# Another order for the first tiles of a hybrid encoder layer, and identity transposes on TensorE at the start

## The reference, cut to what matters

```python
h = rmsnorm(x, norm1_g)
proj = h @ w_in                          # 512 q, 128 k, 128 v, 512 u columns
q = axial_rope(rmsnorm(q, q_norm_g)); k = axial_rope(rmsnorm(k, k_norm_g))
a = attention(q, k, v)                   # 8 query heads, 2 key/value heads of 64, bidirectional
p = multiscale_pool(u, w_pool, pool_scale)      # 4 groups, windows 2, 4, 8, 16
x = x + concat(a, p) @ w_out
x = x + square(relu(rmsnorm(x, norm2_g) @ w_up)) @ w_down
```

## Time and profile before

| | us |
|---|---|
| median of 3 runs | 1545.71 (1545.16 to 1547.87) |
| profiled execution | 1550.65 |
| its span, first to last instruction | 1548.9 |
| PE busy | 1501.4 (97%) |
| DVE, ACT, POOL busy | 1033.5, 730.0, 391.6 |
| mean granted TensorE clock | 0.993 of 2.4 GHz |

### The profile page before, as it was taken

The page is one execution under the profiler, slowest core; times in us unless marked ns, Lnnn a source line. Parts: engine busy times, 40 slices in busy tenths (PEclk is TensorE's granted clock), DMA queues, the critical chain, the costliest instruction groups (busy, mean ns, idle before and its releaser), DMA issues.

```text
span 1548.9 us, 23445 instructions
## 1 busy us (share of the span) xinstructions
PE 1501.4 (97%) x8000; PEld 1333.6 (86%) x8000; DVE 1033.5 (67%) x1290; ACT 730.0 (47%) x1231; POOL 391.6 (25%) x337
## 2 busy tenths in 40 slices
PE   6999989999989998999999999999899999999998
PEld 5999877888868887999999999999688888888887
DVE  6533479999976567544544544447688878888875
ACT  5222269999882344545545545546233223223220
POOL 3432577888870001000000000000222311311300
PEclk9999999999999999999999999999999999999999
DMA  6110011000023745643243243247743443443434
GB/s 232 47 46 17 18 69 45 15 10 14 11 79 123 257 181 214 285 151 134 108 151 134 106 153 134 103 156 268 266 150 95 150 150 102 146 153 105 149 97 175
DMA packets 68789, 193.55 MB, mean 125 GB/s; under 512 B 5504, under 2 KB 7680, under 8 KB 68736
## 3 DMA queue, kind: packets, MB, share of 16 engines
q1 hardware_dynamic: 66832, 181.85, 33.4%
q10 hardware_dynamic: 1904, 11.01, 1.7%
HBM read 120.49 MB, written 67.63 MB: 121 GB/s over the span
## 4 chain that ended last, share of the span: by engine, by line
PE 82%; POOL 5%; DVE 4%; issue 3%; ACT 3%; DMA 2%; SPq 0%; ACTq 0%; POOLq 0%; DVEq 0%
PE ps L736 22%; PE ps L738 21%; PE ps L737 21%; PE ps L933 5%; PE ps L834 3%; PE ps L941 3%; POOL prob L2014 2%; DMA hin<-hd 2%; PE ps L849 1%; PE ps L850 1%; PE ps L816 1%; PE ps L818 1%; PE ps L951 1%; POOL sw_prompt L1957 1%; PE ps L745 1%
## 5 line engine op out<-in xcount | busy, mean ns | idle before, releaser
L736 PE MATMUL ps<-h,wuhi 128*128 128x384 f32 x896 | 300.2, 335 | 5.0 <-issue 3.8
L738 PE MATMUL ps<-h,wulo 128*128 128x384 f32 x896 | 299.9, 335 | 0.0
L737 PE MATMUL ps<-h,wuhi 128*128 128x384 f32 x896 | 299.9, 335 | 0.0
L736 PE MATMUL ps<-wdhi,hidhi 128*128 128x512 f32 x672 | 262.6, 391 | 5.9 <-DVE yacc L1854 5.9
L737 PE MATMUL ps<-wdlo,hidhi 128*128 128x512 f32 x672 | 262.2, 390 | 0.0
L738 PE MATMUL ps<-wdhi,hidlo 128*128 128x512 f32 x672 | 262.1, 390 | 0.0
L1854 DVE TENSOR_TENSOR yacc<-yacc,ps 128x1024 f32<-128x1024 f32 x168 | 204.2, 1217 | 82.5 <-PE ps L738 82.4
L1036 ACT ACTIVATE hidhi<-hin 128x1024 fp32r<-128x1024 f32 (+1 forms) x72 | 86.9, 1207 | 312.0 <-PE ps L738 299.1
L1769 DVE TENSOR_TENSOR u<-u,ps 128x384 f32<-128x384 f32 x96 | 53.1, 553 | 186.3 <-PE ps L738 186.2
L736 PEld LDWEIGHTS ps<-h,wuhi 128*128 128x128 f32 x896 | 168.7, 188 | 5.8 <-issue 5.8
L737 PEld LDWEIGHTS ps<-h,wuhi 128*128 128x128 f32 x896 | 168.7, 188 | 0.0
(11 more groups left out here) (171 smaller groups left out, 2892.7 us busy)
## 6 DMA issues: line engine op xcount, KB each, us to landing
hd<-hout SPq DMA_DIRECT2D x64, 384.0 KB, 3.3
hin<-hd SPq DMA_DIRECT2D x48, 512.0 KB, 3.7
hd<-hout SPq DMA_DIRECT2D x32, 576.0 KB, 2.8
hin<-hd SPq DMA_DIRECT2D x24, 768.0 KB, 4.4
wuraw<-in_w_up SPq DMA_DIRECT2D x17, 1024.0 KB, 6.0
wdraw<-in_w_down SPq DMA_DIRECT2D x8, 2048.0 KB, 9.4
h<-h2d ACTq DMA_DIRECT2D x7, 1536.0 KB, 12.5
xin<-in_x SPq DMA_DIRECT2D x12, 512.0 KB, 3.4
```

Of the source, the lines that this page charges most:

```text
L736: pe.matmul(out, w_hi, m_hi, start=start, stop=False, skip_group_check=resumed)
L737: pe.matmul(out, w_hi, m_lo, start=False, stop=False, skip_group_check=resumed)
L738: return pe.matmul(out, w_lo, m_hi, start=False, stop=stop, skip_group_check=resumed)
```

## The change

- SP: the order becomes x0, ident, w0, g1, w1, w2, w3, x1, w4 to w7, x2, the u columns, gqk, rope, x3, edge, pscale.
- PE: 14 transposes of the identity into an unused part of PSUM before `transpose_x(0)` and 6 behind it. Tile 0's projection (`first_qkv`) goes row by row through q, k and v together, rows 0 to 2 first without the low part of the tile; `transpose_x(1)` moves into it, behind row 4. Tile 1's projection (`second_qkv`) goes into banks 4 and 5, which are those of `project_u`, so it needs not wait for tile 0 to be copied out. `transpose_x(3)` moves from before `project_u(0)` to between its second and third group, `transpose_qk(0)` from there to before the fourth.
- ACT and DVE: rows 0 to 2 of the weights are split before tile 0, rows 4 to 7 before tile 1; the u columns are split in two halves, between the steps of tile 0. The order of the first pair is written out (`first_pair`).
- POOL: the memset of `up` goes between `norm_x(0)` and `norm_x(1)`; for tile 0 the norm of q and k goes before `norm_x(3)`. For tile 1 the order stays.
- The loops over blocks 0 and 1 are written out (Python's `for` instead of `Fori`) on PE, ACT, DVE and POOL.

```diff
+    def load_wi(k):
+        sp.dma_start(wraw[:, k, 0:QKVW], w_in[k * P:(k + 1) * P, 0:QKVW]).then_inc(w_in_in[k], 16)
     sp.dma_start(xin[:, 0], x[0:P]).then_inc(x_in[0], 16)
+    sp.dma_start(ident[:], ident_d).then_inc(ident_in, 16)
+    load_wi(0)
     sp.dma_start(g1b[:], g1.partition_broadcast(P)).then_inc(g1_in, 16)
-    sp.dma_start(ident[:], ident_d).then_inc(ident_in, 16)
-    sp.dma_start(wraw[:, 0, 0:QKVW], w_in[0:P, 0:QKVW]).then_inc(w_in_in[0], 16)
+    for k in range(1, 4):
+        load_wi(k)
     sp.dma_start(xin[:, 1], x[P:2 * P]).then_inc(x_in[1], 16)
-    for k in range(1, KT):
-        sp.dma_start(wraw[:, k, 0:QKVW], w_in[k * P:(k + 1) * P, 0:QKVW]).then_inc(w_in_in[k], 16)
-        if k == 4:
-            load_x(2, 0)
+    for k in range(4, KT):
+        load_wi(k)
+    load_x(2, 0)
     for k in (0, KT // 2):
         sp.dma_start(wraw[:, k:k + KT // 2, QKVW:],
                      w_in[k * P:(k + KT // 2) * P, QKVW:].rearrange("(k p) n -> p k n", p=P)
                      ).then_inc(w_u_in[k // (KT // 2)], 16)
-    load_x(3, 1)
     sp.dma_start(gqkb[:], gqk.partition_broadcast(P)).then_inc(gqk_in, 16)
     sp.dma_start(rope[:, 0], rope_d[0]).then_inc(rope_in[0], 16)
     sp.dma_start(rope[:, 1], rope_d[1]).then_inc(rope_in[1], 16)
+    load_x(3, 1)
...
+    def first_qkv():
+        outs = ((ps[:, 2, :], 0, 512), (ps[:, 3, 0:QKVW - 512], 512, QKVW))
+        def high(k):
+            pe.wait_ge(wi_hi, k + 1)
+            for out, c0, c1 in outs:
+                pe.matmul(out, hThi[0][:, k, 0:P], wihi[:, k, c0:c1], start=k == 0, stop=False)
+        def cross(k):
+            for out, c0, c1 in outs:
+                pe.matmul(out, hTlo[0][:, k, 0:P], wihi[:, k, c0:c1], start=False, stop=False)
+        def low(k):
+            pe.wait_ge(wi_lo, k + 1)
+            for out, c0, c1 in outs:
+                mm = pe.matmul(out, hThi[0][:, k, 0:P], wilo[:, k, c0:c1], start=False, stop=k == KT - 1)
+            return mm
+        pe.wait_ge(hT_hi, 1)
+        for k in range(3):
+            high(k)
+            low(k)
+        pe.wait_ge(hT_lo, 1)
+        for k in range(3):
+            cross(k)
+        for k in range(3, KT):
+            high(k)
+            cross(k)
+            if k == 4:
+                transpose_x(1)
+            mm = low(k)
+        mm.then_inc(qkv_done, 1)
+    def second_qkv():
+        outs = ((ps[:, 4, :], 0, 512), (ps[:, 5, 0:QKVW - 512], 512, QKVW))
+        pe.wait_ge(hT_hi, 2)
+        for k in range(KT):
+            for out, c0, c1 in outs:
+                pe.matmul(out, hThi[0][:, k, P:2 * P], wihi[:, k, c0:c1], start=k == 0, stop=False)
+                pe.matmul(out, hThi[0][:, k, P:2 * P], wilo[:, k, c0:c1], start=False, stop=False)
+        pe.wait_ge(hT_lo, 2)
+        for out, c0, c1 in outs:
+            for k in range(KT):
+                mm = pe.matmul(out, hTlo[0][:, k, P:2 * P], wihi[:, k, c0:c1], start=False, stop=k == KT - 1)
+        mm.then_inc(qkv_done, 1)
+    def first_block():
+        transpose_x(0)
+        warm(6)
+        first_qkv()
+        second_qkv()
+        transpose_x(2)
+        def between(g):
+            if g == 2:
+                pe.wait_ge(v_lo, FIRST + 2)
+                transpose_x(3)
+            if g == 3:
+                transpose_qk(0, 0)
+        pe.wait_ge(qk_copied, FIRST + 2)
+        project_u(0, 0, between)
+        transpose_qk(1, 1)
+        project_qkv(2, 2)
+        transpose_x(4)
+        project_qkv(3, 3)
+        transpose_x(5)
+        project_u(1, 1, lambda g: transpose_qk(2, 2) if g == 2 else None)
+        transpose_qk(3, 3)
     def project_u(p, buf, between):
         pe.wait_ge(u_saved, FIRST + p)
-        pe.wait_ge(wi_u_lo, KT)
         for g in range(GROUPS):
             between(g)
             c0 = QKVW + g * P
             for k in range(KT):
+                if p == 0 and g == 0:
+                    pe.wait_ge(wi_u_lo, k + 1)
...
+    def warm(n):
+        for _ in range(n):
+            pe.transpose(psw[:, 3072:3072 + P], ident[:], ident[:])
     pe.wait_ge(ident_in, 16)
-    transpose_x(0)
-    transpose_x(1)
-    with pe.Fori(0, NB - 1) as n:
+    warm(14)
+    first_block()
+    for n in range(1, NB - 1):
         project_block(n, False)
...
     square_x(0, 0)
-    split_wi(0)
+    for k in range(3):
+        split_wi(k)
+    split_hT(0, 0)
+    split_wi(3)
     square_x(1, 1)
-    split_hT(0, 0)
-    for k in range(1, 3):
+    for k in range(4, KT):
         split_wi(k)
     split_hT(1, 1)
-    for k in range(3, 6):
-        split_wi(k)
     square_x(2, 0)
-    for k in range(6, KT):
-        split_wi(k)
-    for k in range(KT):
+    for k in range(KT // 2):
         split_wi_u(k)
...
+    def first_pair():
+        copy_qkv(0, 2)
+        square_qk(0)
+        for k in range(KT // 2, KT):
+            split_wi_u(k)
+        square_x(3, 1)
+        copy_qkv(1, 4)
+        split_hT(2, 2)
+        square_qk(1)
+        split_hT(3, 3)
+        square_x(4, 0)
+        save_qkT(0)
+        save_u_columns(0, 1)
+        save_qkT(1)
...
     dve.wait_ge(g1_in, 16)
     scale_x(0, 0)
-    split_wi(0)
+    for k in range(3):
+        split_wi(k)
+    split_hT(0, 0)
+    split_wi(3)
     scale_x(1, 1)
-    split_hT(0, 0)
-    for k in range(1, 3):
+    for k in range(4, KT):
         split_wi(k)
     split_hT(1, 1)
-    for k in range(3, KT):
-        split_wi(k)
     scale_x(2, 0)
-    for k in range(KT):
-        split_wi_u(k)
-    dve.wait_ge(gq_scaled, 1)
...
+    def first_pair():
+        split_v(0, 3)
+        sum_squares(0)
+        for k in range(KT // 2):
+            split_wi_u(k)
+        dve.wait_ge(gq_scaled, 1)
+        norm_qk(0)
+        for k in range(KT // 2, KT):
+            split_wi_u(k)
+        split_v(1, 5)
+        split_hT(2, 2)
+        scale_x(3, 1)
+        sum_squares(1)
+        rotate(0, 0)
+        norm_qk(1)
+        split_hT(3, 3)
+        rotate(1, 1)
+        scale_x(4, 0)
...
     norm_x(0)
+    pool.memset(up[:], 0.0).then_inc(pads, 1)
     norm_x(1)
     norm_x(2)
     pool.wait_ge(gqk_in, 16)
     pool.tensor_scalar(gqkb[:, 0:NQ], gqkb[:, 0:NQ], SCALE, 1.0, ALU.mult, ALU.mult
                        ).then_inc(gq_scaled, 1)
-    pool.memset(up[:], 0.0).then_inc(pads, 1)
...
+            opens = isinstance(n, int) and t == 0
+            if not (last and i >= 1) and not opens:
                 norm_x(t + 3)
             pool.wait_ge(qk_summed, FIRST + t + 1)
             pool.wait_ge(qn_done, FIRST + t)
             rsqrt_mean(rsqk[:], msqk[:], ssqk[:], epsqk[:], msqk_done, rsqk_done, FIRST + t)
+            if opens:
+                norm_x(3)
...
-    with pool.Fori(0, NB - 1) as n:
+    for n in range(NB - 1):
         project_block(n, False)
```

More of the change, by code:

```diff
@@ L756, in project_qkv @@
                     for k in range(KT):
-                        if i == 0 and c0 == 0:
-                            pe.wait_ge(wi_lo, k + 1)
                         mm = three(out, hThi[buf][:, k, tok:tok + P], hTlo[buf][:, k, tok:tok + P],
@@ L1111, in exps, with copy_qkv, square_qk @@
                 ins.then_inc(exp_done, 1)
+            def copy_qkv(t, bank):
+                act.wait_ge(qkv_done, t + 1)
+                act.wait_ge(qn_done, FIRST + t)
+                copy(qk[:].rearrange("p h d -> p (h d)"), psw[:, bank * 512:bank * 512 + QKW]).then_inc(qk_copied, 1)
+                copy(V[:, bass.ds(t, 1), :, 0:HEAD].rearrange("p a v d -> p (a v) d"),
+                     ps[:, bank + 1, P:2 * P].rearrange("p (v d) -> p v d", v=NKV)).then_inc(v_hi, 1)
+            def square_qk(t):
+                act.wait_ge(qk_copied, FIRST + t + 1)
+                act.wait_ge(qk_summed, FIRST + t)
+                act.activation(qksq[:], qk[:], ACT.Square, scale=HEAD ** -0.5).then_inc(qk_squared, 1)
@@ new lines, in save_u_columns @@
+            def save_u_columns(n, i):
+                p = n * 2 + i // 2
+                act.wait_ge(u_done, FIRST + p + 1)
+                act.wait_ge(pads, 1)
+                copy(up[:, :, bass.ds(p * 256 + PAD + 2 * PAD * ((n + 1) // 2), 256)],
+                     psw[:, 2048:3072].rearrange("p (g c) -> p g c", g=GROUPS)).then_inc(u_saved, 1)
+            def first_pair():
[12 more added lines that the diff above has]
+                save_qkT(1)
@@ L1113, in project_block @@
             def project_block(n, last):
-                for i in range(4):
+                for i in range(2 if isinstance(n, int) and n == 0 else 0, 4):
                     t = n * 4 + i
[L1116 to L1124, removed]
+                    copy_qkv(t, 2)
+                    square_qk(t)
@@ L1147, in project_block @@
                     if i % 2:
[L1148 to L1152, removed]
+                        save_u_columns(n, i)
                         save_qkT(t)
-            with act.Fori(0, NB - 1) as n:
+            first_pair()
+            for n in range(NB - 1):
                 project_block(n, False)
```

(37 more changed lines are left out.)

## The result

| | before | changed |
|---|---|---|
| median, 12 runs each | 1546.11 (1543.92 to 1548.10) | 1550.57 (1548.29 to 1553.61) |
| ratio to the kernel before | | 1.0022, 95% interval 1.0013 to 1.0030 |
| profiled execution, its span | 1550.65, 1548.9 | 1549.51, 1547.7 |

The change makes the kernel slower by 2.0 to 4.6 us, 3.4 by the ratio (the medians lie 4.5 apart). That is 0.2% of the time: small, but clear of the noise. The two profiled executions stand the other way round, 1.1 us apart; the one of before was slower than all 12 runs of that kernel. So the first stage is compared moment by moment, and the whole by medians.

The account below looks back on a forecast made before the run. PE, busy for 97% of the span, was taken as the bound. The shift of transpose_qk(1), -0.1 us, plus 1.5 us of half rate behind the pause gave +1.4: 1545.71 to 1547.1 us, range 1543.5 to 1550.5.

Parts of the forecast that it names:

- rival 1: Clock low at PE's first matmul: +2.5 us, 1548.2; with longer half rate behind the pause +4.2, 1549.9; chance 0.25.
- The first matmul: Start of PE's first projection: at 12.45 instead of 16.19, 3.7 us earlier; bounds 11.8 and 13.0.
- g1's landing: Load that gates scale_x(0): lands between about 7.0 and 8.65, taken as 8.2.
- The clock at the first matmul: PE's first projection: the sum assumed full rate, with 20 identity transposes keeping PE occupied for most of 5 to 12.
- transpose_x(3): PE's transposes of x tile 3, after two groups of project_u(0): start at 37.15, against 36.67 before.
- u wait: PE waiting for the last u split, which ends at 33.9, ahead of transpose_x(3): 0.3 us.
- The chain: Steps across engines from transpose_x(3) to transpose_qk(1): 12.33 us, lower end 11.4; transpose_qk(1) at 49.5, PE still for 5.2.
- POOL's power: POOL's step in the norm of q and k of tile 1: 2.88 us taken, which goes with a DVE that waits.
- The half rate behind the pause: Matmuls behind the pause ahead of transpose_qk(1) run at half rate: 1.5 us added once, range 0 to 3.4.
- The sum: Whole kernel: -0.1 + 1.5 = +1.4 us, from the median 1545.71 to 1547.1.
- Rival 2: The chain behind transpose_x(3) doesn't hold PE; transpose_qk(1) comes at 44.3: -5.3 us, 1540.4; chance 0.10.

Follow-up runs that it names:

- e1: Changed kernel with POOL's norm of q and k ahead of the norm of x for tile 1 too; 1544.57 us, ratio 0.9989 to before.
- e8: Changed kernel with 36 identity transposes filling the pause ahead of transpose_qk(1); 1548.98 us, ratio 1.0011 to before.
- e9: Changed kernel with its first four loads in the order x0, g1, ident, w0; 1550.88 us, ratio 1.0028 to before.
- e4: Changed kernel with 34 instead of 14 identity transposes ahead of transpose_x(0); 1551.49 us, ratio 1.0027 to before.
- e5: Changed kernel with e1's order, e4's transposes, and POOL's wait for edge and pscale moved to the last block; 1545.79 us, ratio 0.9985 to before.
- e6: e5 with tile 1's squares of q and k summed before tile 2 is split; 1543.78 us, ratio 0.9974 to before.
- e7: Changed kernel with its first four loads in the order x0, ident, g1, w0; 1549.75 us, ratio 1.0017 to before.
- e10: e6 with gqk's load ahead of the u columns; 1545.04 us, ratio 0.9990 to before.
- e2: Changed kernel without its 20 identity transposes; 1550.72 us, ratio 1.0020 to before.
- e3: Kernel before with its loops over blocks 0 and 1 written out on PE, ACT, DVE and POOL; 1545.27 us, ratio 0.9997.

## Why the prediction was right, and where not

It forecast slower, by 1.4 us, because the head start would end in a pause ahead of transpose_qk(1) with half rate behind it. This is what happened, shown by e1 (take the chain away, and the kernel is faster than before) and e8 (fill the pause, and half rate goes). The size is another matter. The median of 1550.57 lies 3.5 over the 1547.1 forecast and just outside the stated range (1543.5 to 1550.5), and +3.4 by the ratio is more than the forecast's own branch allowed (1548.5 is +2.8). It lies between the two sizes of rival 1 (+2.5 and, by its own terms, +4.3; it has 4.2), which had a chance of 0.25. So the direction was reasoned, and the branch that came true was the first rival's. Step by step:

- **The first matmul**: 12.45 forecast, 11.8 to 13.0 its bounds, 13.81 measured: outside. The failed step is g1's landing, taken as 8.2 and bounded by 8.65, since the same four transfers had landed by then. It was 9.39. The bound had left out that their order matters; e9 shows it with 6.85, and with the order of the change the four took 0.7 us longer in all.
- **The clock at the first matmul**: the sum had it at full rate, rival 1 at half. Rival 1 came true, full rate from about 15.7. Its reason, that transposes raise nothing, did not: the Trainium skill's rule ("TensorE: Matmul & The Clock Gate", Part 4, PE-mode transpose: a transpose does not count as busy in the way a matmul does) is contradicted by e4 and e8. What stood in the way was most likely the 3.0 us without work between the last of the fourteen and x tile 0. The traces with transposes sort by this gap: 0 to 2.0 us (e4, e5, e6, e7, e9, e10), and the first matmul is at full rate; 3.0 to 3.8 us (changed kernel, e1, e8), and it is at half rate. In e7 it is the same fourteen with 2.0 us behind them, and x tile 0 took 1.09 instead of 1.97. No run changed the gap alone.
- **transpose_x(3)**: 37.15 forecast, 38.2 in rival 1, 39.13 measured. The 1.4 us of the late start and 0.95 of half rate, less the 0.3 of u wait that did not come, make it up.
- **The chain**: 12.33 forecast, 11.4 its lower end, 50.45 - 39.13 = 11.32 measured. POOL's power took 1.96, where I had taken 2.88; the reason given for 2.88, a DVE that waits, failed, for DVE waited 4.88 us there. Two errors of opposite sign: transpose_qk(1) was due at 49.5 and came at 50.45, a pause of 4.0 for 5.2.
- **The half rate behind the pause**: 1.5 forecast with 3.4 as upper end. It took 1.3 in the profiled run. The distances from q1 to x4 give 1.3, 1.6, 1.6, 2.7 and 2.6 us in the changed kernel, e2, e4, e7 and e9, which all have the pause of 4.0: about 2.0 a run. The term was taken 0.5 too small.
- **The sum**: +1.4 forecast; the ratio says +3.4 (2.0 to 4.6). By the traces 1.0 of the 2.0 between them lies ahead of q1 (+0.9 for -0.1: the two steps at the start) and 0.5 behind the pause; the remaining 0.5 is within the interval. The clocks of the runs divide the +3.4 otherwise, 0.3 of waits and work and 3.1 of half rate, but with their errors the two do not contradict each other. In the two profiled runs the half rate adds up to 10.3 us before and 13.7 in the changed kernel: 1.7 of the difference is the stretch at the pause, 1.7 a stretch at 612 to 620 that lasted twice as long. Whether the latter is the shift's doing or chance is not settled.
- The memset, the splits of the weight rows and the loops cost nothing that shows: e3 for the last; for the others, PE has no wait from x tile 0 to q1. The forecast's one hidden wait, the last u split (0.3 us), turned into the next bound as soon as PE came earlier (e4 to e7, e9).
- Rival 2, the head start survives, is out as the change stands. e1 and e6 show what of it was to be had: not 5.3 but 1.7 and 4.0 us by the ratios, and e6 has three edits more than e1.

## What to carry to other kernels

A head start is worth what the next cross-engine chain lets through. Before moving work forward on the busiest engine, find its next wait that is now met with no slack, and ask which instruction of the same engine that chain begins with. Here it was transpose_x(3), which the change moved back behind two groups of `project_u`, and one norm in front of another on a third engine held the chain for 4.2 us. And a pause costs more than its length when the matmul engine's clock falls in it: reorder to remove it, or fill it.

## What the runs showed of the hardware

- Identity transposes alone raise TensorE's clock (34 of them in e4: the next eight transposes took 1.08 us instead of 1.97) and hold it through a gap of 4.1 us (36 of them in e8: granted clock 1.00 instead of 0.50). 14, followed by 3.0 us of nothing, left the first matmuls at half rate; followed by 2.0 us (e7), they did not.
- A pause of 4.0 us cost another 1.3 to 2.7 us behind it, at a granted clock of 0.50 (1.2 GHz); with one of 1.0 us (e1) nothing followed.
- 64 KB in rows of 512 bytes, loaded ahead of a 512 KB broadcast, delayed the broadcast: there by 6.4 (before) and by 6.85 at the latest (e9) without, at 8.5 (e7) with it, and at 9.4 (changed kernel) with it and 384 KB of weights.
- POOL's power on 128x10 took 1.96 to 2.9 us for the same shape in different surroundings; what decides it was not tried.
- The clock column reads 1.00 before the first recorded transition, while the matmuls' spacing of 0.43 us for 512 columns shows half rate.
